# Moving the areas of the moving operands by unused margins in SBUF

## The chip, the core and the metric

The program runs on one core of one Trainium2 chip. The metric is the device time of one launch in microseconds (us). The kernel before was run twice outside the profiler: 2869.28 and 2871.47 us, median 2870.38 us.

## What is computed

The reference is a chain of two transformer blocks on 256 tokens of width 2048, all in float32, followed by a last normalization. The first block has a modulation from a condition vector, low-rank latent attention with keys of 256 tokens and 256 context tokens, short convolutions, and a gated feed-forward part with a convolution. The second has two kinds of attention, gates, and a squared-relu feed-forward part of width 8192. Nearly all of its arithmetic lies in products of an activation with a weight matrix:

```python
# first block
q, kv, conv = split_projection(h @ w_in[l])          # 2048 x 3904
x = x + gt_a * merge_heads(att, conv, g_mix_out[l], w_out[l])
u = dwconv3(h @ w_up, cw, cb)                        # 2048 x 11008
a, g = jnp.split(u, 2, axis=-1)
x = x + gt_f * ((a * jax.nn.silu(g)) @ w_down)       # 5504 x 2048
# second block
z = hn @ w_in                                        # 2048 x 10248
merged = jax.nn.sigmoid(g_a) * (a @ w_proj_a) + jax.nn.sigmoid(g_b) * (bfx @ w_proj_b)
x = x + merged @ w_out
x = x + jnp.square(jax.nn.relu(hm @ w_up)) @ w_down  # 2048 x 8192 and back
```

## The kernel before

**Layout.** Activations are held transposed: 128 features on the partitions, and for each tile of 128 features one run of 256 tokens along the partition. For accuracy in the fast float32r form, each activation and each weight is split into a rounded part and a remainder ("hi" and "lo"). Of an activation tile `k`, `x[:, k, 0:T]` holds the rounded tokens and `x[:, k, T:2 * T]` the remainder, so a tile is 2048 bytes of each partition, and its two parts begin 1024 bytes apart.

**Weights.** SP issues DMAs of 512 KB (two tiles of 128 x 512 weights) into a ring of eight slots, `raw`. ScalarE copies a slot rounded into one of four slots of `whi` (line 511), VectorE subtracts and writes the remainder into `wlo` (line 909). Each slot has 4096 bytes of a partition.

**Products.** `product` (line 1633) goes over eight such chunks of two tiles. For each tile and each of four blocks of 128 output features, `block` (lines 1627 to 1629) issues three matmuls, with 128 columns of weights as the stationary operand and 256 tokens of the activation as the moving one: hi times hi, hi times lo, lo times hi. So a chunk is 24 matmuls and a product of 2048 by 512 is 192. Every matmul loads its own weights: the trace has a weight load (PEld) for each. `token_product` (lines 1661 to 1663) has the roles the other way round: the activation is stationary and 512 columns of weights move. Each engine runs its own fixed list, and semaphores tie them; a product waits for `wlo` of its chunk and, at its start, for a free half of PSUM.

**Addresses.** Areas of SBUF are handed out one after the other within nested scopes, and areas of scopes that are closed are handed out again. Every residue below is the area's first byte in a partition modulo 512. Tiles (2048 bytes), their two parts (1024) and blocks of weights (512) are whole multiples of 512, so the residue of an area is that of each operand in it. In the kernel before, `whi` and `wlo` begin at residue 128, and all the following at residue 320: `h1`, `hctx`, `mix`, `hf`, `h2`, `hid0`, `hid1`, `heads2_0`, `heads2_1`, `merged`, and `stage` and `acc` of the first stages. `qn` and `kvn`, the small low-rank operands, begin at 64; `ident_sb` and `ones` at 128, `sq` at 160.

**Which product reads which area, and how many matmuls of 256 columns that is.** From the loops of the code, at 192 for a full product: `hf` 7200 (w_up of both blocks), `h2` 3072 (w_in_2 apart from the values), `hid0` 2832 and `hid1` 2304 (w_down of both blocks), `h1` 1488, `heads2_0` and `heads2_1` 768 together, `merged` 768, `mix` 768, `hctx` 144, `qn` 192, `kvn` 96. The profile leaves the digits of names out: its `h` is `h1` and `h2`, its `hid` is `hid0` and `hid1`, its `heads` both of `heads2`.

Of the kernel before, what the change touches and what calls it, by code (L numbers as in the profile page):

```python
# [8 lines left out]
P = 128  # L9
D = 2048  # L10
T = 256
# [14 lines left out]
HT = 16  # L26
# [6 lines left out]
F32R = mybir.dt.float32r  # L33
# [136 lines left out]
def program(nc, ins, consts, out, known, traced):  # L170
    with ExitStack() as ctx:
        def sb(name, shape, dt=F32, scope=ctx):
            return scope.enter_context(nc.sbuf_tensor(name, shape, dt))
# [92 lines left out]
        square_sum = sb("square_sum", [P, TB, 4])  # L266


        first = ExitStack()
        t16 = sb("t16", [P, KT, T], scope=first)  # L270
        krope = sb("krope", [P, 2 * T], scope=first)
        acc = sb("acc", [P, NACC, GW], scope=first)
        sc = ExitStack()
        stage = sb("stage", [P, 4, D], scope=sc)
        cst = sb("cst", [P, KT, P], F32R, scope=sc)
# [3 lines left out]
        sc = ExitStack()  # L279
# [9 lines left out]
        sc = ExitStack()  # L289
# [15 lines left out]
        sc = ExitStack()  # L305
# [4 lines left out]

        sc = ExitStack()
        hf = sb("hf", [P, KT, 2 * T], F32R, scope=sc)
        hid = [sb(f"hid{i}", [P, HT, 2 * T], F32R, scope=sc) for i in range(2)]
        sc.close()


        sc = ExitStack()
        h2 = sb("h2", [P, KT, 2 * T], F32R, scope=sc)
        heads2 = [sb(f"heads2_{i}", [P, HEADS, 2 * T], F32R, scope=sc) for i in range(2)]
        sc2 = ExitStack()  # L320
        q2 = sb("q2", [P, 2, 4, T], scope=sc2)
        k2 = sb("k2", [P, 2, 4, T], scope=sc2)
# [11 lines left out]
        sc = ExitStack()  # L334
# [1711 lines left out]
```

## Time and profile before

| | |
|---|---|
| median of two runs | 2870.38 us (2869.28 to 2871.47) |
| the profiled execution, its own time | 2872.42 us |
| its span, first to last instruction | 2870.6 us |
| TensorE matmul busy (PE) | 2684.6 us, 94% |
| TensorE weight load busy (PEld) | 2571.9 us, 90% |
| VectorE busy | 1794.6 us, 63% |
| ScalarE busy | 1224.7 us, 43% |
| share of the chain that ended last, TensorE | 86% |
| granted TensorE clock, mean | 0.959 |

A matmul's duration in the trace reaches from its start to its modelled end and overlaps the next ones. So its mean duration says little of the pace; the pace is read from start to start, or as matmuls in a window over its length, less the two or so that were under way when the window began.

### The profile page before, as it was taken

How to read it: one execution, taken by the hardware profiler on the slowest of the kernel's cores; microseconds unless marked ns; L12 is line 12 of the kernel's file. 1: busy time of each engine (PE TensorE's matmuls, PEld its weight loads, DVE VectorE, ACT ScalarE, POOL GpSimd, SP SyncE). 2: the span in 40 equal slices, each digit the busy share in tenths (PEclk: the TensorE clock that was granted, in tenths of full speed). 3: DMA queues.
4: the chain of work that ended last, by engine and by line, in shares of the span. 5: the costliest groups of instructions: out<-in, count | busy, mean ns of one | idle time of the engine just before them, and what ended most of it. 6: DMA issues, size and time to landing. Idle time of an engine off the chain costs nothing.

```text
span 2870.6 us, 52211 instructions
## 1 busy us (share of the span) xinstructions
PE 2684.6 (94%) x21408; PEld 2571.9 (90%) x21408; DVE 1794.6 (63%) x2056; ACT 1224.7 (43%) x1407; POOL 20.8 (1%) x24
## 2 busy tenths in 40 slices
PE   4959977768899999999999999999999999999998
PEld 3659975348899999999999999999999999999998
DVE  3988965678766776576556455555555555555554
ACT  2733331223455554354454344444444443434433
POOL 0000000000000000000000000000000000000000
PEclk9989987769999999999999899999999999999999
DMA  4958953427566656656556455566556666666562
GB/s 156 384 195 315 331 171 120 147 88 282 188 191 201 195 182 204 192 163 220 183 171 186 130 173 166 161 188 199 196 178 184 191 197 192 190 196 193 196 206 103
DMA packets 288834, 552.93 MB, mean 193 GB/s; under 512 B 19434, under 2 KB 28632, under 8 KB 288024
## 3 DMA queue, kind: packets, MB, share of 16 engines
q1 hardware_dynamic: 287416, 548.10, 59.2%
q8 instruction: 125, 2.05, 0.3%
q10 hardware_dynamic: 1248, 2.42, 0.3%
q14 instruction: 45, 0.37, 0.0%
HBM read 548.35 MB, written 2.10 MB: 192 GB/s over the span
## 4 chain that ended last, share of the span: by engine, by line
PE 86%; DVE 9%; issue 2%; ACT 2%; DMA 1%; ACTq 1%; DVEq 0%; SPq 0%
PE half L1627 25%; PE half L1629 25%; PE half L1628 25%; DVE wlo L909 2%; PE half L1683 1%; DVE acc L931 1%; PE half L1661 1%; PE half L1663 1%; DVE acc L928 1%; PE half L1662 1%; DVE tmp L1233 1%; DMA raw<-in_w_ada 1%; PE half L1832 1%; PE half L1821 1%; PE half L1822 1%
## 5 line engine op out<-in xcount | busy, mean ns | idle before, releaser
L909 DVE TENSOR_TENSOR wlo<-raw,whi 128x1024 fp32r<-128x1024 f32 (+2 forms) x917 | 1096.7, 1209 | 815.8 <-ACT whi L511 813.6
L511 ACT ACTIVATE whi<-raw 128x1024 fp32r<-128x1024 f32 (+2 forms) x917 | 952.5, 1048 | 1195.0 <-PE half L1629 1033.6
L1627 PE MATMUL half<-hf,whi 128*128 128x256 f32 x2400 | 663.9, 277 | 6.2 <-DVE hf L986 5.1
L1628 PE MATMUL half<-hf,whi 128*128 128x256 f32 x2400 | 663.4, 276 | 0.0
L1629 PE MATMUL half<-hf,wlo 128*128 128x256 f32 x2400 | 663.4, 276 | 0.0
L1627 PE MATMUL half<-hid,whi 128*128 128x256 f32 x1712 | 474.0, 277 | 0.0
L1628 PE MATMUL half<-hid,whi 128*128 128x256 f32 x1712 | 473.4, 276 | 0.0
L1629 PE MATMUL half<-hid,wlo 128*128 128x256 f32 x1712 | 473.4, 276 | 0.0
L1627 PEld LDWEIGHTS half<-hf,whi 128*128 128x128 f32 x2400 | 451.4, 188 | 7.0 <-issue 5.5
L1629 PEld LDWEIGHTS half<-hf,wlo 128*128 128x128 f32 x2400 | 451.3, 188 | 0.0
L1628 PEld LDWEIGHTS half<-hf,whi 128*128 128x128 f32 x2400 | 451.2, 188 | 0.0
L1627 PE MATMUL half<-h,whi 128*128 128x256 f32 x1520 | 430.5, 283 | 21.1 <-issue 15.9
L1628 PE MATMUL half<-h,whi 128*128 128x256 f32 x1520 | 426.7, 281 | 0.0
L1629 PE MATMUL half<-h,wlo 128*128 128x256 f32 x1520 | 426.5, 281 | 0.0
L1627 PEld LDWEIGHTS half<-hid,whi 128*128 128x128 f32 x1712 | 321.6, 188 | 0.1
L1629 PEld LDWEIGHTS half<-hid,wlo 128*128 128x128 f32 x1712 | 321.6, 188 | 0.0
L1628 PEld LDWEIGHTS half<-hid,whi 128*128 128x128 f32 x1712 | 321.5, 188 | 0.1
L1627 PEld LDWEIGHTS half<-h,whi 128*128 128x128 f32 x1520 | 289.9, 191 | 21.6 <-issue 15.9
L1628 PEld LDWEIGHTS half<-h,whi 128*128 128x128 f32 x1520 | 290.6, 191 | 0.3
L1629 PEld LDWEIGHTS half<-h,wlo 128*128 128x128 f32 x1520 | 290.8, 191 | 0.0
L1627 PE MATMUL half<-mix,whi 128*128 128x256 f32 x256 | 74.0, 289 | 30.2 <-DVE tmp L1233 17.4
L931 DVE SCALAR_TENSOR_TENSOR acc<-raw,silu_sb,acc 128x512 f32<-128x512 f32 x128 | 96.2, 752 | 4.5
(253 smaller groups left out, 3092.0 us busy)
## 6 DMA issues: line engine op xcount, KB each, us to landing
raw<-in_w_up SPq DMA_DIRECT2D x288, 512.0 KB, 4.4
raw<-in_w_in SPq DMA_DIRECT2D x216, 512.0 KB, 4.1
raw<-in_w_down SPq DMA_DIRECT2D x212, 512.0 KB, 4.1
raw<-in_w_ada SPq DMA_DIRECT2D x192, 512.0 KB, 5.7
raw<-in_w_out SPq DMA_DIRECT2D x64, 512.0 KB, 4.7
raw<-in_w_proj_a SPq DMA_DIRECT2D x16, 512.0 KB, 3.7
raw<-in_w_proj_b SPq DMA_DIRECT2D x16, 512.0 KB, 4.2
raw<-in_w_up SPq DMA_DIRECT2D x16, 384.0 KB, 3.5
```

What stands on the lines that cost most here:

```text
L511: A(whi[:, s, 0:elems], raw[:, c, 0:elems], ACT.Copy).then_inc(s_hi_ready, 1)
L909: V.tensor_tensor(wlo[:, s, 0:elems], raw[:, c, 0:elems], whi[:, s, 0:elems].bitcast(F32), ALU.subtract).then_inc(s_drained, 1)
L928: V.scalar_tensor_tensor(a, w[:, 0, :], s[:, 0:1], a, ALU.mult, ALU.add).then_inc(s_dve_step, 1)
L931: V.scalar_tensor_tensor(a, w[:, 1, :], s[:, 1:2], a, ALU.mult, ALU.add).then_inc(s_drained, 1)
L1233: ins_ = V.reciprocal(flat(tmp), flat(tmp))
L1627: mm(o, hi, x[:, 0:T], start=(k == 0 and b % 2 == 0), stop=False, skip_group_check=True)
L1628: mm(o, hi, x[:, T:2 * T], start=False, stop=False, skip_group_check=True)
L1629: return mm(o, lo, x[:, 0:T], start=False, stop=(k == nk - 1), skip_group_check=True)
L1661: mm(o, xh, hi, start=(k == 0), stop=False)
L1662: mm(o, xh, lo, start=False, stop=False)
L1663: ins_ = mm(o, xl, hi, start=False, stop=(k == nk - 1))
L1683: ins_ = mm(half()[:, 0, 0:width], ones[:], sq[:, j % 2, b * width:(b + 1) * width], start=(c + b == 0), stop=(c == chunks - 1 and b == pe ...
```

## The change

Five tensors that nobody reads or writes are allocated, and move what is allocated behind them (the fourth and the fifth stand in place of the third and the second in another scope, so there are four places). No instruction is added, removed or put in another place; on every engine the order and the shapes are those of before.

```diff
         square_sum = sb("square_sum", [P, TB, 4])
 
 
+        sb("margin", [P, 112])
+
         first = ExitStack()
         t16 = sb("t16", [P, KT, T], scope=first)
         krope = sb("krope", [P, 2 * T], scope=first)
         acc = sb("acc", [P, NACC, GW], scope=first)
+        sb("margin_first", [P, 104], scope=first)
         sc = ExitStack()
...
         hf = sb("hf", [P, KT, 2 * T], F32R, scope=sc)
-        hid = [sb(f"hid{i}", [P, HT, 2 * T], F32R, scope=sc) for i in range(2)]
+        sb("margin_hid0", [P, 16], scope=sc)
+        hid = [sb("hid0", [P, HT, 2 * T], F32R, scope=sc)]
+        sb("margin_hid1", [P, 120], scope=sc)
+        hid.append(sb("hid1", [P, HT, 2 * T], F32R, scope=sc))
         sc.close()
 
 
         sc = ExitStack()
         h2 = sb("h2", [P, KT, 2 * T], F32R, scope=sc)
+        sb("margin_heads", [P, 16], scope=sc)
         heads2 = [sb(f"heads2_{i}", [P, HEADS, 2 * T], F32R, scope=sc) for i in range(2)]
+        sb("margin_merged", [P, 120], scope=sc)
```

| area | first byte before | modulo 512 | first byte after | modulo 512 |
|---|---|---|---|---|
| `whi`, `wlo` | 65664, 82048 | 128 | the same | 128 |
| `hf`, `h2`, `t16` | 124736 | 320 | 125184 | 256 |
| `hid0`, `heads2_0` | 157504 | 320 | 158016 | 320 |
| `heads2_1` | 173888 | 320 | 174400 | 320 |
| `hid1`, `merged`, `q2` | 190272 | 320 | 191264 | 288 |
| `h1`, `mix`, `stage` | 151360 | 320 | 152224 | 160 |
| `hctx`, `cst` | 184128 | 320 | 184992 | 160 |
| `qn` | 202816 | 64 | 203680 | 416 |
| `kvn` | 211008 | 64 | 211872 | 416 |
| `acc` | 143168 | 320 | 143616 | 256 |

## Rows read from the trace of the kernel before

**Rows 1.** The page: busy time by engine, and the chain's shares.
```profile
PE 2684.6 (94%) x21408; PEld 2571.9 (90%) x21408; DVE 1794.6 (63%) x2056; ACT 1224.7 (43%) x1407; POOL 20.8 (1%) x24
PE 86%; DVE 9%; issue 2%; ACT 2%; DMA 1%; ACTq 1%; DVEq 0%; SPq 0%
```
**Rows 2.** Windows, TensorE: bounds, length, busy (matmuls), clock, DMA share, GB/s.
```profile
228.00:251.00 23.00, 23.00 (x206) 1.00 0.93 328
1900.00:2000.00 100.00, 100.00 (x885) 1.00 0.64 195
2400.00:2500.00 100.00, 100.00 (x885) 1.00 0.63 193
```
**Rows 3.** The same view, stretches with the longer pace.
```profile
176.00:228.00 52.00, 46.84 (x379) 0.95 0.60 187
251.00:274.00 23.00, 23.00 (x197) 1.00 1.02 369
303.00:373.00 70.00, 68.64 (x581) 0.99 0.99 353
703.00:726.00 23.00, 23.00 (x198) 1.00 1.00 360
1436.00:1494.00 58.00, 58.00 (x455) 1.00 0.61 182
1559.00:1586.00 27.00, 27.00 (x223) 1.00 0.55 172
2099.00:2172.00 73.00, 73.00 (x601) 1.00 0.56 175
2827.00:2856.00 29.00, 29.00 (x249) 1.00 0.00 1
```
**Rows 4.** Timeline of TensorE, nine matmuls apart, `merged` and `hf`: start, duration, instruction.
```profile
2099.83 0.28 PE L1629 MATMUL half<-merged,wlo 128*128 128x256 f32 x1
...
2100.89 0.28 PE L1629 MATMUL half<-merged,wlo 128*128 128x256 f32 x1
...
2199.82 0.28 PE L1627 MATMUL half<-hf,whi 128*128 128x256 f32 x1
2199.82 0.19 PEld L1628 LDWEIGHTS half<-hf,whi 128*128 128x128 f32 x1
...
2200.84 0.28 PE L1627 MATMUL half<-hf,whi 128*128 128x256 f32 x1
```
**Rows 5.** Timeline of TensorE around a small side product at 250.5 us.
```profile
250.54 0.94 PE L1597 MATMUL half<-ones,acc 128*128 128x1 f32 x8
251.35 0.36 PE L1627 MATMUL half<-h,whi 128*128 128x256 f32 x1
```
**Rows 6.** Timeline of TensorE: transposes at 37.5 us.
```profile
37.53 1.15 PE L1702 MATMUL half<-ident_sb,stage 128*128 128x128 f32 x9
```
**Rows 7.** Timeline of TensorE at 438 us, at half of the clock.
```profile
438.24 0.41 PE L1629 MATMUL half<-kvn,wlo 128*128 128x256 f32 x1
438.45 0.41 PE L1627 MATMUL half<-kvn,whi 128*128 128x256 f32 x1
```
**Rows 8.** Groups of instructions of TensorE: busy us, mean ns.
```profile
L1628 PE MATMUL half<-merged,whi 128*128 128x256 f32 x256 | 71.4, 279 | 0.0
L1628 PE MATMUL half<-heads,whi 128*128 128x256 f32 x256 | 70.7, 276 | 0.0
```
**Rows 9.** The same view, within 421 to 427 us.
```profile
L1627 PE MATMUL half<-qn,whi 128*128 128x256 f32 x19 | 5.2, 276 | 0.0
```
**Rows 10.** Windows by stage, all engines: the up and down products of both blocks.
```profile
760.00:1430.00 670.00, 668.89 (x5894) 668.49 (x5893) 440.84 (x526) 333.74 (x380) 0.00 (x0) 1.00 0.60 189
2172.00:2800.00 628.00, 628.00 (x5541) 627.95 (x5541) 350.32 (x291) 274.24 (x262) 0.00 (x0) 1.00 0.62 195
```
**Rows 11.** Waits, longest in total first: who waited for whom, us, times, longest.
```profile
ACT whi L511 <- PE half L1629: 1033.6, 629, 8.7
PE half L1627 <- DVE wlo L909: 17.3, 4, 12.8
```

## The prediction

> **What bounds the kernel now.** I read the page first. TensorE is busy for 2684.6 of 2870.6 us and holds 86% of the chain that ended last [rows 1]. The other engines are far from it: VectorE 63%, ScalarE 43%. The waits say the same from the other side. ScalarE waits 1033.6 us in total for a slot that TensorE has finished with, while TensorE's large group waits only 17.3 us for split weights [rows 11]. In the two long stages of the feed-forward parts TensorE is busy without a break (668.9 of 670 us, 628 of 628 us), VectorE for 440.8 and 350.3 us of them, the DMA share is 0.60 and 0.62 [rows 10]. So the time is the number of matmuls times the pace from one start to the next. A change that moves nothing in the order can act through that pace alone.
>
> The windows give the pace. From 2400 to 2500 us, in `hid` and `hf`, and from 1900 to 2000 us, in `h2` and `heads`, there are 885 matmuls each [rows 2]; less the two or so under way at a window's start, 883 in 100 us give 113.3 ns. Nine starts of `hf` say the same: 2200.84 - 2199.82 = 1.02 us, 113.3 ns each. There is a second level. Nine starts of `merged` take 2100.89 - 2099.83 = 1.06 us, 117.8 ns each [rows 4], and from 251 to 274 us there are 197 matmuls of `h1` where the 23 us before held 206, eight very short ones among them [rows 2, 3]. I call them the short and the long pace; they differ by 4.4 ns, and the granted clock is 1.00 in both, the upper of the two levels, 2.4 GHz. At half of that clock the matmuls of the same shape start every 0.21 us [rows 7], and 0.213 us is 256 columns at 1.2 GHz: there is no excess there. At the full clock 256 columns would be 106.7 ns, so the short pace carries 6.7 ns more and the long one 11.1 ns.
>
> Each matmul has a weight load of its own, which starts within 0.01 us of the matmul before [rows 4]. The moving operand is thus read while the next weights are read, for the same stretch of time. Were the pace a matter of where the two reads stand in SBUF, it would depend on the residues, and that is the only thing the change alters.
>
> **The change, part by part.** The five margins add no instruction, no DMA and no wait. The DMAs of the weights write to `raw`, which does not move; ScalarE and VectorE write hi and lo parts at moved places, in the same lengths, and they have 30% to 50% of the time in hand [rows 10], so any cost to them is nothing as long as that cover stands. `hid0` and the two `heads2` keep residue 320: 3600 matmuls in which I expect no change of their own. The moved ones are `hf` and `h2` with 7200 + 3072 = 10272, `hid1` and `merged` with 2304 + 768 = 3072, and `h1`, `mix`, `hctx` with 1488 + 768 + 144 = 2400; 15744 in all, besides 288 of `qn` and `kvn`. `token_product` has 512 columns for each load and its activation is stationary; it has 384 matmuls, and I leave it at its present pace.
>
> What does the residue do to the pace? The trace bounds it from both sides.
>
> The best case is a pace of 109 ns: nine transposes, which read 128 columns from `stage` at 320 and load 128 columns each, take 1.15 us with the last one's 0.28 us: 0.87 / 8 = 109 ns [rows 6]. So a load every 109 ns is possible. The gain would be 4.3 ns from the short pace for each matmul. The worst that this trace shows is the long pace, 4.4 ns more.
>
> Two facts speak for no dependence on the residue, at least between these two levels. `h1` at residue 320 runs in the short pace from 228 to 251 us and in the long one from 251 to 274 us [rows 2, 3], in the same product, with the same areas. What stands between the two is a side product of eight matmuls of one column [rows 5]. So the level is picked by how the stream of loads and moving reads happens to be aligned in time after an interruption, and it stays until the next one. And `qn` at residue 64 has the 276 ns of duration that go with the short pace [rows 9], as `heads` has at 320 [rows 8]. One fact speaks for a dependence: two levels, lasting for hundreds of matmuls, look like two streams that meet at a fixed place in each period; if they meet in SBUF, then moving one by 32 to 352 bytes moves that place, and the long pace may vanish or spread.
>
> The Trainium skill, "TensorE: Matmul & The Clock Gate", step 1 of its part on issuing a matmul, says that TensorE has two independent read ports into SBUF, and that loading the next weights takes no read bandwidth from the running matmul. By that rule the residues do nothing and the time stays at 2870 us. That rule alone does not explain two paces at one clock, so the trace neither confirms nor refutes it.
>
> So my sum is this. The two levels remain, and the share of the long one changes. The long stretches of rows 3, with three more of `h2` like the one at 1559 us (the last ends at 1833 us), hold about 3600 matmuls: 3600 x 4.4 ns = 16 us is all that the long pace costs. Of these, about 260 between 1436 and 1474 us read `hid0`, which keeps its residue. About 980 lie where the DMA share is 0.99 to 1.02 at 353 to 369 GB/s [rows 3], and there a faster TensorE would wait for weights instead: what is late next is the DMA. That leaves 2360 x 4.4 ns = 10 us to be won, if all of them go over to the short pace. I take 7 us, between nothing and the 16 us, since alignment is drawn anew after each interruption, and now from streams that meet elsewhere. From the profiled execution's own time: 2872.4 - 7 = 2865.4 us. The median of the runs shown is 2.0 us below that execution, so I forecast **2863 us**. The case as such reaches from 2854 us (all 16 us) to 2876 us.
>
> **The rivals.**
>
> *Nothing at all changes*, the mechanism lies within TensorE and its timing is independent of addresses: the same stretches are long, to the matmul, and the time is 2870 us. For it: the switch of level without any change of area. I cannot tell it from my forecast by the verdict, only by the trace; the two together have 0.60, this one 0.25.
>
> *The residues free the loads.* The pace of the moved areas falls toward 109 ns. In `hf`, `h2`, `hid1` and `merged`: 13344 x 4.3 ns = 57 us, and 7 us of the long stretches in `h2`, `merged` and `hid1`; the DMA share in those stages, 0.6, leaves room for a pace 4% faster. 2870.4 - 64 = 2806 us. Only `hf` and `h2`: 44 us, 2826 us. Against it: 15000 matmuls at 320 and 64 show no sign of any pace between 109 and 113. I give 0.14 to the full form, 0.08 to the partial one, together with anything between 2826 and 2854 us. The same page of the Trainium skill, section "Back-to-back issue gap", gives N / 2.4 + 2.5 ns for a matmul of N columns at the full clock, which is 109.2 ns for 256; it is the same as my row for transposes, and by it the excess of 4.1 ns is something that can be taken away.
>
> *The move makes the long pace the rule.* The two streams now meet where it costs more. For residues 288 and 160, which are multiples of 32 but not of 64 as 320 and 256 are, that is 5472 matmuls, of which about 2180 are long already (the first four stretches of rows 3, the last, and three products of `merged`): 3290 x 4.4 = +15 us, 2885 us (0.10). For all moved areas: 15744 - 3340 = 12400 x 4.4 = +55 us, 2925 us. The place of it would be the weight load, longer by 4.4 ns in every matmul of `hf`. It decides from the point where the streams fall out of step in a loop without interruptions, since there they stay so: `hf` has over 4500 in a row. To be slower by over 2% it takes a third level, 4.6 ns or more above the short one in all areas. 0.08 for these forms together, of which 0.04 beyond 2%.
>
> **How the numbers follow.** Forecast 0.35, nothing 0.25, partial gain 0.08, full gain 0.14, partial loss 0.10, full loss 0.08. Two per cent, what a measurement of this kernel can tell from no change, is 57 us: below 2813 or above 2928 us. Faster by over 2%: the full gain, 0.14. Slower by over 2%: 0.04. Within: 0.82. For the range I take in the partial forms on both sides, 2826 to 2888 us, and leave out the two full ones, 0.22.
>
> **What would show it.** In the trace after, the windows of rows 2 keep 883 matmuls per 100 us in `hf`; at 109 ns they would hold 917, at the long pace 849. `heads`, which keeps its residue, should stay at 276 ns of mean duration whatever happens [rows 8]; a move of it would say that the cause is not the residue of the moving operand. `merged`, 279 ns now since most of it is long, tells at once whether its level changed. If TensorE becomes faster, waits for `wlo` and DMA near 251 to 373 us should grow. I am wrong if the levels themselves move: a pace in `hf` other than 113.3 or 117.8 ns means that the residue sets the cost of each load, and not just the draw between two alignments.

## The result, and the profile after

The changed kernel takes 2938.99 us (2936.92 and 2941.05 in two runs), against 2870.38 us before: the ratio is 1.024, with a 95% interval of 1.020 to 1.028. In four more runs beside the kernel before the ratio was 1.023 (1.022 to 1.025). It is slower by 2.4%. The forecast was 2863 us, with a range up to 2888 us.

The page of the changed kernel, its busy time by engine and the chain's shares, as [rows 1]:

```profile
PE 2753.9 (94%) x21408; PEld 2641.1 (90%) x21408; DVE 1796.9 (61%) x2056; ACT 1224.7 (42%) x1407; POOL 22.4 (1%) x24
PE 86%; DVE 8%; issue 2%; ACT 1%; DMA 1%; ACTq 1%; DVEq 0%; SPq 0%
```

The chain line reads the same except for a point each of VectorE and ScalarE. TensorE is busy for 69.3 us more with the same 21408 matmuls, VectorE and ScalarE are as before. The span grew by 68.7 us. So each matmul came later, and no new wait appeared: ScalarE only waits longer for TensorE, as [rows 11]:

```profile
ACT whi L519 <- PE half L1637: 1098.4, 635, 8.9
DVE wlo L917 <- ACT whi L519: 877.8, 583, 13.3
```

The windows, as [rows 2, 3] (bounds, length, busy and count, clock, DMA share, GB/s). For the first of them the kernel before has this line:

```profile
780.00:1100.00 320.00, 320.00 (x2826) 1.00 0.61 192
```

And the changed kernel has these:

```profile
780.00:1100.00 320.00, 320.00 (x2699) 1.00 0.59 183
1130.00:1200.00 70.00, 70.00 (x620) 1.00 0.62 193
2240.00:2360.00 120.00, 120.00 (x1002) 1.00 0.63 183
2475.00:2555.00 80.00, 80.00 (x677) 1.00 0.62 185
2567.00:2647.00 80.00, 80.00 (x684) 1.00 0.59 187
1947.00:1962.00 15.00, 15.00 (x130) 1.00 0.64 184
```

Less the two or so under way at a window's start, the first row of the changed kernel is 320 us / 2697 = 118.7 ns: `hf`, now at residue 256, where the kernel before has 320 / 2824 = 113.3 ns. The second is `hid0`, which kept 320: 70 / 618 = 113.3 ns, the short pace of before. Then `hf` in another stretch, 120 / 1000 = 120.0 ns, the same by its starts; `hf` at 118.7 by its starts again, 80 / 675 in a window with a change of product; and `hid1` at 288, 80 / 682 = 117.3 ns. The last row lies within one product of `heads`, at the old 320, 117.8 ns by its starts. The granted clock is 1.00 in each of them.

Nine starts of `hf`, as [rows 4]: 2500.88 - 2499.81 = 1.07 us, where it was 1.02 us; the weight load starts with the matmul before, as it did.

```profile
2499.81 0.28 PE L1635 MATMUL half<-hf,whi 128*128 128x256 f32 x1
2499.81 0.19 PEld L1636 LDWEIGHTS half<-hf,whi 128*128 128x128 f32 x1
...
2500.88 0.28 PE L1635 MATMUL half<-hf,whi 128*128 128x256 f32 x1
```

The mean durations, as [rows 8]. `hf` had 276 to 277 ns before; `heads` has gone from 276 to 279 though its residue is the old one.

```profile
L1635 PE MATMUL half<-hf,whi 128*128 128x256 f32 x2400 | 678.5, 283 | 5.9 <-DVE hf L994 5.1 <-DVE wlo L917 0.8
L1636 PE MATMUL half<-merged,whi 128*128 128x256 f32 x256 | 71.9, 281 | 0.0
L1636 PE MATMUL half<-heads,whi 128*128 128x256 f32 x256 | 71.3, 279 | 0.0
```

Taking for every matmul of the three lines the time from its start to the next start (those over 126 ns, which hold a wait or another product, left out), the loss by area is the number of matmuls times the difference of the mean paces:

| area | matmuls | residue before, after | mean pace before, after (ns) | loss (us) |
|---|---|---|---|---|
| `hf` | 7200 | 320, 256 | 113.4, 118.9 | 39.6 |
| `h2` | 3072 | 320, 256 | 114.8, 119.0 | 12.9 |
| `hid0` and `hid1` | 5136 | 320, 320 and 288 | 113.8, 115.5 | 8.7 |
| `merged` | 768 | 320, 288 | 115.8, 118.7 | 2.2 |
| `mix` | 768 | 320, 160 | 114.6, 117.3 | 2.1 |
| `heads` | 768 | 320, 320 | 113.4, 115.6 | 1.7 |
| `h1`, `hctx`, `qn`, `kvn` | 1920 | 320 or 64, 160 or 416 | | 1.2 |

The sum is 68.4 of the 68.7 us of the span. `h1` cost next to nothing: much of it had been in the long pace, with a mean of 116.4 ns, and its new mean is 116.7 ns.

### The profile page after: what moved, and what is told of

It reads as the page before. It is cut to its first block, busy times and chain, and to the rows that moved or that the text cites. A ratio compares the mean times of both kernels' runs of the same rounds, so it can differ in the third digit from the quotient of the medians.

```text
span 2939.3 us, 52211 instructions
## 1 busy us (share of the span) xinstructions
PE 2753.9 (94%) x21408; PEld 2641.1 (90%) x21408; DVE 1796.9 (61%) x2056; ACT 1224.7 (42%) x1407; POOL 22.4 (1%) x24
## 4 chain that ended last, share of the span: by engine, by line
PE 86%; DVE 8%; issue 2%; ACT 1%; DMA 1%; ACTq 1%; DVEq 0%; SPq 0%
PE half L1635 25%; PE half L1637 25%; PE half L1636 25%; DVE wlo L917 2%; PE half L1691 1%; PE half L1669 1%; PE half L1671 1%; PE half L1670 1%; DVE acc L939 1%; DVE acc L936 1%; DVE tmp L1241 1%; DMA raw<-in_w_ada 1%; PE half L1840 1%; PE half L1829 1%; PE half L1830 1%
## 5 line engine op out<-in xcount | busy, mean ns | idle before, releaser
L1635 PE MATMUL half<-hf,whi 128*128 128x256 f32 x2400 | 678.5, 283 | 5.9 <-DVE hf L994 5.1
L1636 PE MATMUL half<-hf,whi 128*128 128x256 f32 x2400 | 677.9, 282 | 0.0
L1637 PE MATMUL half<-hf,wlo 128*128 128x256 f32 x2400 | 677.9, 282 | 0.0
L1635 PE MATMUL half<-h,whi 128*128 128x256 f32 x1520 | 434.9, 286 | 21.1 <-issue 15.9
L1636 PE MATMUL half<-h,whi 128*128 128x256 f32 x1520 | 431.1, 284 | 0.0
```

The costliest lines, as they stand in the source:

```text
L1635: mm(o, hi, x[:, 0:T], start=(k == 0 and b % 2 == 0), stop=False, skip_group_check=True)
L1636: mm(o, hi, x[:, T:2 * T], start=False, stop=False, skip_group_check=True)
L1637: return mm(o, lo, x[:, 0:T], start=False, stop=(k == nk - 1), skip_group_check=True)
```

## The experiments

From here on, *distance* is the residue of the moving operands less that of the split weights. It was 192 before (320 - 128), and -64 for `qn` and `kvn`. The change makes it 128 for `hf` and `h2`, 160 for `hid1` and `merged`, 32 for `h1` and `mix`. The theory: the pace depends on this distance. The rivals: the residue of the moving operand alone; the mere fact of moving; the mixture of residues; a timing that has nothing to do with addresses.

**control512: everything moved, all residues kept.**

```diff
+        sb("margin", [P, 128])
```

> One margin of 512 bytes ahead of all the areas, so that every address behind it moves and every residue modulo 512 stays that of the kernel before (320, weights at 128). If the residue is the cause (distance theory and moving-address theory alike): the same paces, 113.3 ns and the long 117.8 ns in the same stretches, 2870 us. If it is the absolute place, or that anything was moved at all: something between 2880 and 2940 us.

Measured: ratio 1.000 (0.998 to 1.003). Its ten runs lie in two groups, seven from 2869 to 2878 us and three from 2889 to 2895 us. So do those of the kernel before on that chip, 13 runs with three near 2892 us. The profiled one is of the upper group, and shows what that group is:

```profile
780.00:1100.00 320.00, 320.00 (x2719) 1.00 0.59 186
2440.00:2510.00 70.00, 70.00 (x620) 1.00 0.64 192
```

The first stretch of `hf`, short in the trace before, is in the long pace here (320 / 2717 = 117.8 ns), and later `hf` is short, at 113.3 ns. The mean of `hf` is 115.8 ns instead of 113.4 ns, which is 17 us, and the draw was made once, at the start of a stretch of some 4600 matmuls of `hf` and `hid`. Moving as such costs nothing.

**weights_only: the split weights moved by 64 bytes, the moving operands left.**

```diff
+        sb("margin_whi", [P, 16])
         whi = sb("whi", [P, NSPLIT, CW], F32R)
         wlo = sb("wlo", [P, NSPLIT, CW], F32R)
+        sb("margin_vec", [P, 112])
```

The second margin keeps the residue of everything behind the weights.

> Only the split weights move, by 64 bytes, to 192 modulo 512; all moving operands stay at 320. Distance theory (what counts is how far the moving operand starts from the weights, modulo a small power of two): the distance is 128, as it is for hf at 256 in the changed kernel, so nearly all of the 16,000 matmuls in the short pace go from 113.3 to about 118.7 ns: +85 us, 2955 us. Moving-address theory (the residue of the moving operand alone counts, and 320 is a good one): 2870 us.

Measured: 2959.08 us, ratio 1.028 (1.024 to 1.032).

```profile
780.00:1100.00 320.00, 320.00 (x2699) 1.00 0.59 183
2390.00:2465.00 75.00, 75.00 (x635) 1.00 0.55 183
```

The first row is to the matmul the count that `hf` has in the changed kernel: 118.7 ns at distance 128, here with `hf` itself unmoved. `hid`, in the second, is the same, 75 / 633, 118.7 ns by its starts. The moving operand's own residue is refuted as the cause.

**both_moved: both by 64 bytes, distance 192.** As weights_only, with a further margin of 64 bytes ahead of the areas.

> Split weights at 192 and all moving operands at 384: both are moved by 64 bytes, the distance of 192 is that of the kernel before. Distance theory: 2870 us, 113.3 ns. Moving-address theory: 384 is a multiple of 128 as the bad 256 is, so about 118.7 ns nearly everywhere and 2955 us.

Measured: 2904.70 us median, 2900.70 at the lowest, ratio 1.011 (1.006 to 1.016).

```profile
780.00:1100.00 320.00, 320.00 (x2826) 1.00 0.61 191
2345.00:2425.00 80.00, 80.00 (x682) 1.00 0.59 185
```

The short pace is back (320 / 2824 = 113.3 ns), at a residue of 384, a multiple of 128 that the rival called bad. But from 2156 us on all is in the long pace, 117.8 ns, for 700 us. By the paces that is 25 us more than in the kernel before, most of the 30 us by which 2870 us was missed. All four runs were above 2900 us, so it is not the draw of a single run. The distance restores the two levels, not their shares. The share of the long pace is not a function of the distance alone, and what else picks it stays open.

**only_hf: only `hf` and `h2` at distance 128.** The change's first margin, and margins that take the rest back to 320.

> Of the change only the first part: hf and h2 at 256 (distance 128 from the weights), every other area at 320 (distance 192). Distance theory: hf and h2 at 118.7 to 119.9 ns as in the changed kernel, the rest at 113.3 or 117.8; from the changed kernel's paces hf costs 40 us and h2 13 us over the kernel before, so 2923 us, three quarters of the whole loss. Rival (the loss comes from the mixture of four different residues in one program): well under 2900 us.

Measured: 2935.03 us, ratio 1.022 (1.020 to 1.023): nearly all of the loss, and 12 us above the 2923 us expected. By the paces `hf` costs 39.8 us and `h2` 12.6 us, as expected.

```profile
780.00:1100.00 320.00, 320.00 (x2699) 1.00 0.58 183
1130.00:1200.00 70.00, 70.00 (x621) 1.00 0.61 193
2210.00:2370.00 160.00, 160.00 (x1329) 1.00 0.63 184
```

The other 9 us come from areas that kept 320: `hid` 4.1, `mix` 2.1, `heads` 1.7, `h1`, `merged` and `qn` about 2 us. They fell more often into the long pace. `heads` has 115.6 ns, as in the changed kernel: its four stretches follow products of `h2` at 118.7 or 120.0 ns, and two of them run at 117.8 ns from their start, where all four had 113.3 ns before. So the cost of a bad distance reaches into neighbours that kept theirs. That they inherit an alignment from the product ahead is my reading and not shown; in the run `fine` below, `heads` follows products of `h2` at 119.2 ns and is at 113.4 ns in all four stretches.

**after_again: the changed kernel beside the kernel before.** No edit.

> The changed kernel once more, beside the kernel before on the same chip, because the kernel before has shown two groups of times, near 2872 and near 2891 us, that go with the level which the first stretch of hf falls into. Theory: at distances other than 192 there is no short pace to fall out of, so the changed kernel spreads less, within some 8 us around 2939 us. Rival (both kernels draw alike): a second group some 20 us away.

Measured: 2934.77 to 2943.82 us, ratio 1.023 (1.022 to 1.025). No second group in four runs, which is too few to exclude one: 5 of 40 runs of the kernel before on the chips of these experiments, and six of 20 runs of control512 and minus64, were above 2889 us. Its profile differs from the first one of this kernel in one main point: the first `hid0` stretch, still at 320, was in the long pace, 117.8 ns.

**map_a and map_b: other distances by area.** Only the sizes of the margins differ.

> Weights at 128; hf and h2 at 192 (distance 64), hid0 and heads2 at 224 (distance 96), hid1 and merged at 128 (distance 0), h1 and mix at 352 (distance 224). A map of paces by area. If only the distance modulo 128 counts: hf and h2 at 113.3 ns (64 is as good as 192), hid1 and merged as 128 is in the changed kernel, 118.7 ns. If it counts modulo 256 or more, hf may differ from 113.3 ns, and distance 0 from distance 128. The odd multiples of 32 lie between, 116.5 to 118.5 ns. If the residue of the moving operand alone counts modulo 128: the same for hf (192 is 64 modulo 128), so this run does not tell the two apart.

> Weights at 128; hf and h2 at 448 (distance 320), hid0 and heads2 at 384 (distance 256), hid1 and merged at 480 (distance 352), h1 and mix at 0 (distance -128). If the distance counts modulo 256: hf as at distance 64, 117.8 ns and never 113.3; hid0 and heads as at 0, 120.0 ns; hid1 and merged as at 96, 119.95 ns; h1 as at 128, near 119. If it counts modulo 512, these values need not return. If it counts modulo 128: hf would also show the short pace of 113.3 ns in some stretches.

Measured in single runs: 2953.30 and 2957.11 us. Of map_a, the windows hold `hf` at distance 64, then `hid0` at 96, `hid1` at 0:

```profile
780.00:1100.00 320.00, 320.00 (x2719) 1.00 0.60 186
2390.00:2470.00 80.00, 80.00 (x669) 1.00 0.57 183
2572.00:2652.00 80.00, 80.00 (x669) 1.00 0.56 181
```

Of map_b, `hf` at 320 (64 modulo 256), `hid0` at 256 (0), `hid1` at 352 (96):

```profile
780.00:1100.00 320.00, 320.00 (x2720) 1.00 0.59 186
2393.00:2473.00 80.00, 80.00 (x669) 1.00 0.57 183
2576.00:2656.00 80.00, 80.00 (x669) 1.00 0.57 182
```

Distance 64 is 117.8 ns and distances 0 and 96 are 80 / 667 = 120.0 ns, each twice, 256 bytes apart. My expectation for map_a, 113.3 ns for `hf` by a period of 128, was wrong: 64 is not as good as 192. My expectation for map_b held for all of `hf`, `hid` and `h1` (118.9 ns at -128), with one exception: in two of the stretches of `h2` some 70 of 384 matmuls were at 113.3 ns. So distance 64 has the short pace too, though rarely, and "never" was too much.

**minus64: all moving operands at 64, distance -64.**

```diff
+        sb("margin", [P, 64])
```

> Weights at 128, all moving operands at 64: distance -64, which is 192 modulo 256 but 448 modulo 512. If the distance counts modulo 256: the paces of the kernel before, 113.3 ns and 117.8 ns after some interruptions, 2870 us, or near 2891 us where the first stretch of hf falls into the long one. If it counts modulo 512: another pace, above 116.5 ns everywhere, 2925 us or more.

Measured: 2872.90 us, ratio 1.001 (0.998 to 1.004).

```profile
780.00:1100.00 320.00, 320.00 (x2826) 1.00 0.61 191
2170.00:2320.00 150.00, 150.00 (x1318) 1.00 0.65 190
```

The first stretch of `hf` is at 113.3 ns; the second window, in which a side product stands too, has the count of 1318 that the kernel before has in the same bounds, and 113.4 ns by its starts. With map_a and map_b this shows the period of 256 bytes from its best and its worst places.

**both_32: weights at 160, moving operands at 352, distance 192.**

> Weights at 160 and all moving operands at 352: distance 192 again, but both begin at odd multiples of 32. Distance theory: 113.3 ns and 117.8 ns, 2870 to 2891 us. Rival (each must also begin at a multiple of 64): above 116.5 ns everywhere, 2925 us or more.

Measured: 2875.91 us in one run, among those of the kernel before.

```profile
780.00:1100.00 320.00, 320.00 (x2826) 1.00 0.61 191
2170.00:2320.00 150.00, 150.00 (x1319) 1.00 0.64 192
```

Neither operand needs a multiple of 64: the two levels come back with the distance.

**fine: steps below 32 bytes.** The areas are views into slightly larger tensors.

```diff
+            at = off % 512 // 4
+            t = sb(name, [P, k * 2 * T + 128], F32R, scope=scope)
+            return t[:, at:at + k * 2 * T].rearrange("p (k t) -> p k t", k=k)
...
-        hf = sb("hf", [P, KT, 2 * T], F32R, scope=sc)
-        hid = [sb(f"hid{i}", [P, HT, 2 * T], F32R, scope=sc) for i in range(2)]
+        hf = sb_off("hf", KT, -16, sc)
+        hid = [sb_off(f"hid{i}", HT, ((16), (-8))[i], sc) for i in range(2)]
```

> Offsets below 32 bytes around the good distance of 192: hf and h2 at 304 (distance 176), hid0 at 336 (208), hid1 at 312 (184), h1 and mix at 328 (200); merged and heads2 stay at 320. If 192 is the middle of a basin: 184 and 200 are 113.3 or a little lower, 176 and 208 between 113.3 and 117.3 ns. If a read is served in units of 32 bytes: 176 is as 160 (117.3 ns) and 208 as 192 (113.3 ns). If only multiples of 64 give a steady pace: all four irregular, 115 to 119 ns.

Measured: 2960.68 us in one run. `hf` at distance 176, `hid0` at 208, `hid1` at 184:

```profile
780.00:1100.00 320.00, 320.00 (x2686) 1.00 0.58 182
2396.00:2476.00 80.00, 80.00 (x673) 1.00 0.57 184
2579.00:2659.00 80.00, 80.00 (x669) 1.00 0.57 182
```

They are at 119.3, 119.2 and 120.0 ns, and `h1` at 200 has 120.0 ns. All three of my pictures fail. The basin and the units of 32 bytes: eight bytes off 192 is as bad as anything measured. The third, that all four would be irregular at 115 to 119 ns: at 184 and 200 the starts are even, nearly all from 119 to 121 ns, and all four lie above 119 ns.

**without_hf: the change without its first part.** Margins of 352 bytes (`margin_first`) and 480 bytes (`margin_hid1`, `margin_merged`) alone.

> The change without its first part: hf, h2, hid0 and heads at 320, hid1 and merged at 288, h1 and mix at 160. Distance theory: what the changed kernel lost outside hf and h2, 15 us by its paces, so 2885 us, and up to 20 us more in executions in which the first stretch of hf is in the long pace. Rival (a mixture of residues costs by itself): over 2910 us at its lowest.

Measured: 2884.59 us, ratio 1.003 (1.001 to 1.005), against 2885 us expected.

```profile
780.00:1100.00 320.00, 320.00 (x2826) 1.00 0.60 192
2512.00:2592.00 80.00, 80.00 (x685) 1.00 0.58 188
```

`hf` is at 113.3 ns again, `hid1` at 80 / 683 = 117.1 ns, 117.3 by its starts. The mixture of residues costs nothing by itself. Its ten runs spread from 2878 to 2887 us, without the upper group that I had allowed for.

**wlo_only: one load in three at distance 128.**

```diff
         whi = sb("whi", [P, NSPLIT, CW], F32R)
+        sb("margin_wlo", [P, 16])
         wlo = sb("wlo", [P, NSPLIT, CW], F32R)
+        sb("margin_vec", [P, 112])
```

> Only the remainders of the weights (wlo) move, to 192; rounded weights stay at 128, moving operands at 320. Of three loads one (the one that runs beside the matmul of the second line of block) has distance 128, the other two 192. If what counts is the pair of load and matmul that run at the same time: the start that ends that pair comes late, by about 5 ns, the other two at 113.3 ns, mean 115.1 ns, about 2900 us. Rival (the three cannot be told apart, the alignment of all is lost): all three gaps near 118 ns on average, 2945 us.

Measured: 2951.21 us in one run: the rival's number.

```profile
780.00:1100.00 320.00, 320.00 (x2709) 1.00 0.59 185
```

The mean is 320 / 2707 = 118.2 ns in every area. From 800 to 1000 us the next start comes 119.0 ns after that of the first line of `block`, 119.5 after the second, 116.2 after the third. The second is the one beside which the moved weights are loaded, and it is the latest, but by 0.5 ns only; the first is late as well. A single pair out of step spoils all three.

The map, by starts, distance modulo 256:

| distance | 0 | 32 | 64 | 96 | 128 | 160 | 176 | 184 | 192 | 200 | 208 | 224 |
|---|---|---|---|---|---|---|---|---|---|---|---|---|
| ns | 120.0 | 116.7, 117.8 | 117.8 | 120.0 | 118.7, 120.0 | 117.3, 118.7 | 119.3 | 120.0 | 113.3, 117.8 | 120.0 | 119.2 | 118.3 |

Where two stand, both occur in products of full length; rarer exceptions, such as the 113.4 ns at distance 64, are left out. Distances 176, 184, 200, 208 and 224 come from one run each. No place was found below 113.3 ns, so the experiments point to no kernel better than the one before.

## Why the prediction was wrong

**The frame was right.** TensorE's pace is the bound, the change acts through it alone, the other engines' cover holds, and the clock is 1.00 in the windows that matter. Margins and moved writes cost nothing, as control512 shows. The count of moved matmuls was right. A small term was missed: `token_product`, which I left at its present pace, went from 229.0 to 232.6 ns in the second block, 380 starts or 1.3 us.

**The step that failed** is the one that says "the two levels remain, and the share of the long one changes". In the large moved areas neither level of before remained: `hf` and `h2` went to 118.7 and 120.0 ns, `hid1` and `merged` to 117.3 and 118.7 ns. `h1`, at 160, went to 116.7 ns; only `mix`, at 160 too, is in part at 117.8 ns. The place of the operands sets the pace, and not only the draw between two alignments, which is what the prediction named as the sign of its being wrong. The sum had -7 us for that step, and the runs show +68 us, 52 of them in `hf` and `h2`.

**Two rows misled me, and one was read past its reach.** I took `qn` at 64 with the pace of `hf` at 320 as a sign that the residue does not matter [rows 8, 9]. They differ by 256, which is the period: the trace of before held a single distance twice, and so said nothing on distance. I took the switch of level without a change of area [rows 2, 3, 5] as evidence against the residue. It shows that timing picks between levels at one distance, and it leaves open that the distance sets which levels there are. And I capped the loss at the long pace, "the worst that this trace shows", for every rival but 0.04. A trace at one distance cannot bound the others.

**The rivals.** The one on the slow side had the right mechanism and the right sign, with 15744 matmuls and 4.4 ns. For `hf` the step was 5.5 ns, and its 0.08, with 0.04 for a third level, was too little. It priced 256 as harmless in its partial form ("multiples of 32 but not of 64"), where 256 was the costliest residue of the change. The full gain, toward 109 ns, found no support at any of twelve distances. The rule of the Trainium skill that I weighed ("TensorE: Matmul & The Clock Gate", step 1 of its part on issuing a matmul, two independent read ports) gave 2870 us, and weights_only speaks against it as a rule of time: moving only the weights, by 64 bytes, costs 3%. The 109.2 ns for 256 columns by the same page of the Trainium skill, section "Back-to-back issue gap", was reached nowhere in these products. I had read it past its reach: that section of the Trainium skill gives that formula for the isolated gap of a single matmul, and says that in a stream of pairs of load and matmul both set the spacing.

**The signs.** `merged` told at once, 279 to 281 ns. `heads` was to stay at 276 ns "whatever happens" and went to 279. That did not say that the residue is not the cause: only_hf shows that `heads` changes while its own distance stays, when what runs ahead of it is moved. It was a bad control, since it is not isolated from what was moved.

**What is shown and what is not.** Shown: the distance between moving operand and split weights decides, modulo 256 bytes, which paces occur, for these matmuls of 256 columns that each load new weights, at the full clock. Not shown: what collides. That the two reads meet in SBUF fits the distance. ScalarE and VectorE also write at these places, but the pace does not follow their activity: from 780 to 1100 us in the trace before, with VectorE busy for 225.9 us and ScalarE for 169.1 us of the 320, every start of a matmul is 113 or 114 ns after the one ahead. Still, no run separates the reads from anything else that shares the addresses. Open as well: what picks the short or long pace at distance 192, which moves the kernel before between 2870 and 2892 us, and why it picks the long one more often in both_moved.

## What to carry to other kernels

Where TensorE is the bound and each matmul loads its weights anew, the start of the moving operand relative to the weights was worth 3% to 6% of the matmul's pace here, so note both addresses modulo 256 before and after any change that adds or resizes a tensor ahead of them. A residue taken from a trace in which all operands stand alike proves nothing on other residues: vary it in one run, area by area, before pricing it. And compare kernels of this kind over several executions, since one alignment drawn at the start of a long stretch was worth some 17 us here.

## What the runs showed of the hardware that I had not expected

- A pace that depends on bytes: 113.3 ns at distance 192, 120.0 ns at 184 and at 200. Eight bytes are 6%.
- A mean pace has an even or an uneven form. At distances 0, 184 and 200, and in the short pace at 192, nearly all single starts follow within about 1 ns of the mean; at 64, and in the long pace at 192, within about 2 ns. At the others they are uneven: in map_b the three lines of `hid1` at distance 96 run through gaps from 115 to 125 ns with a mean of 120.0, while every gap of `hid0` at distance 0 is 120 ns.
- The same kernel, with the same clock and no wait, has executions near 2870 and near 2892 us. In the one execution of the upper group whose trace was read (control512), a stretch of some 4600 matmuls runs at 117.8 ns from its first to its last, where the trace before has 113.3 ns.
